# Products of constants in TensorE's known waits: a two-block kernel of hybrid attention, routed experts and a state-space branch

## The reference, cut to what matters

```python
def reference(...):
    x = first_block(...)     # (1, 512, 1024), context of 256 tokens
    return second_block(x, ...)

# first block
mod = silu(c) @ ada_w + ada_b
h = rmsnorm(x, g) * (1 + sc1) + sh1;  u = h @ w_in
a = diff_attention(u);  b = neighbourhood_attention(u);  p = pool_mix(u)
f = hyena_filters(S, w1, b1, w2, b2, w3, b3)
      # sin(z @ w1 + b1); sin(. @ w2 + b2); (. @ w3 + b3) * decay; normed
hy = hyena_mix(u, f)
x = x + g1 * (concat(a, b, p, hy) @ w_out)
h2 = rmsnorm(x, g2) * (1 + sc2) + sh2
x = x + g2 * moe(h2)         # 16 experts, the best 2 of the best group
x = rmsnorm(x, final_g)
# second block
h = rms_norm(x);  q, k, v, za, u, zs, g = split(h @ w_in_2)
attn = windowed_gqa(q, k, v) * silu(za)
ssm = s5_bidirectional(u) -> gelu -> glu -> * silu(zs)
merged = sigmoid(g_a) * (attn @ w_branch_attn) + sigmoid(g_s) * (ssm @ w_branch_ssm)
out = rms_norm(x + merged @ w_out)
```

## Time and profile before

| | us |
|---|---|
| median of 3 runs | 1337.29 |
| lowest and highest run | 1320.17, 1338.97 |
| the profiled execution | 1334.26 |
| its span, first to last instruction | 1332.2 |

### The profile page before, as it was taken

One profiled execution on the slowest core, in us unless ns is written; L12 is line 12 of the kernel. 1 busy time (PEld: TensorE's weight loads), 2 busy tenths in 40 slices (PEclk: granted clock), 3 DMA queues, 4 the chain that ended last, 5 costly groups with the idle time before them and its releaser, 6 DMA issues.

```text
span 1332.2 us, 16908 instructions
## 1 busy us (share of the span) xinstructions
PE 1220.0 (92%) x6412; PEld 899.1 (67%) x6412; DVE 862.2 (65%) x1282; ACT 588.6 (44%) x781; POOL 129.2 (10%) x126
## 2 busy tenths in 40 slices
PE   6999999968799995899999999889999898989996
PEld 1444474857688764788888888648877777765774
DVE  3479788768775447588898888664337555734543
ACT  1540010335555524487777787343333443334422
POOL 1101101000122000011221111300000000000000
PEclk9999999988799997899999999999999899899998
DMA  8735656770130053699999999652343445544301
GB/s 360 279 134 221 237 234 224 182 158 1 56 147 1 0 201 136 237 359 392 408 411 398 408 409 401 247 197 78 110 172 108 145 169 155 167 144 157 126 0 63
DMA packets 52822, 267.52 MB, mean 201 GB/s; under 512 B 15031, under 2 KB 22071, under 8 KB 38040
## 3 DMA queue, kind: packets, MB, share of 16 engines
q1 hardware_dynamic: 38264, 205.85, 42.1%
q0 software_dynamic: 9744, 47.19, 9.8%
q10 hardware_dynamic: 4752, 13.63, 2.7%
HBM read 226.80 MB, written 36.70 MB: 198 GB/s over the span
## 4 chain that ended last, share of the span: by engine, by line
PE 74%; DVE 13%; ACT 5%; DMA 3%; issue 3%; SPq 2%; POOL 1%; DVEq 0%; ACTq 0%; POOLq 0%
PE PS L2772 21%; PE PS L3196 7%; PE PS L3197 7%; PE PS L3198 7%; PE PS L3110 3%; PE PS L3422 3%; PE PS L3423 3%; PE PS L3424 3%; PE PS L3328 2%; PE PS L3327 2%; PE PS L3329 2%; PE PS L3064 2%; PE PS L3408 1%; SPq L804 1%; PE PS L2789 1%
## 5 line engine op out<-in xcount | busy, mean ns | idle before, releaser
L1394 ACT ACTIVATE arena_r<-ring 128x2048 fp32r<-128x2048 f32 x100 | 185.9, 1910 | 11.7 <-ACT arena L1431 7.4
L2772 PE MATMUL PS<-arena 128*128 128x64 f32 (+6 forms) x674 | 150.1, 390 | 30.0 <-DMA arena<-in_small_f_w 7.6
L2223 DVE TENSOR_TENSOR arena_r<-ring,arena_r 128x2048 fp32r<-128x2048 f32 x66 | 148.2, 2286 | 20.3 <-ACT arena_r L1394 19.7
L2772 PEld LDWEIGHTS PS<-arena 128*128 128x128 f32 (+2 forms) x674 | 100.2, 205 | 73.9 <-issue 40.5
L2772 PE MATMUL PS<-hT,ring 128*128 128x512 f32 (+1 forms) x304 | 118.9, 549 | 0.0
L3196 PE MATMUL PS<-arena_r,hT_r 128*128 128x512 f32 x272 | 112.4, 413 | 4.9 <-DVE hT_r L2405 4.9
L3422 PE MATMUL PS<-arena_r 128*128 128x512 f32 x256 | 104.7, 409 | 13.0 <-DVE ring_r L2631 8.5
L3197 PE MATMUL PS<-arena_r,hT_r 128*128 128x512 f32 x272 | 108.9, 400 | 0.0
L3424 PE MATMUL PS<-arena_r,ring_r 128*128 128x512 f32 x256 | 101.8, 398 | 0.0
L1203 ACT ACTIVATE arena<-PS 128x1024 f32<-128x1024 f32 (+2 forms) x31 | 28.5, 927 | 159.7 <-PE PS L2772 144.7
L2772 PEld LDWEIGHTS PS<-hT,ring 128*128 128x128 f32 x304 | 57.1, 190 | 59.0 <-issue 57.4
(11 more groups left out here) (481 smaller groups left out, 2416.0 us busy)
## 6 DMA issues: line engine op xcount, KB each, us to landing
ring<-in_moe SPq DMA_DIRECT2D x51, 2048.0 KB, 10.5
ring<-in_slabs SPq DMA_DIRECT2D x27, 2048.0 KB, 8.9
ring<-in_slabs SPq DMA_DIRECT2D x9, 1024.0 KB, 5.5
y_rows<-arena ACTq DMA_DIRECT2D x16, 512.0 KB, 10.0
ssm_scratch<-arena POOLq DMA_DIRECT2D x4, 1152.0 KB, 5.1
arena<-ssm_scratch POOLq DMA_DIRECT2D x4, 1152.0 KB, 8.3
ssm_scratch<-arena POOLq DMA_DIRECT2D x4, 1024.0 KB, 10.9
y_rows<-in_tab_no_token SPq DMA_DIRECT2D x1, 4096.0 KB, 25.1
```

The costliest lines, as they stand in the source:

```text
L1394: nc.scalar.activation(rounded(moe_w_hi[n][:, cols]), ring[:, n, cols], ACT.Copy).then_inc(s_moe_hi[n], 1)
L2223: nc.vector.tensor_tensor(rounded(moe_w_lo[n][:, cols]), ring[:, n, cols], as_float(moe_w_hi[n][:, cols]), ALU.subtract).then_inc(s_moe_lo ...
L2772: ins = nc.tensor.matmul(out, lhsT, rhs, start=(n == 0), stop=(n == len(pairs) - 1))
```

## The change

A helper issues `n` plain 32-bit products of `ones` by `vec` (256 columns) into a bank that is free at that point and is written anew by what follows. It is called ahead of waits of TensorE: before the second and the third filter layer (8, 4), before the list (7), before the first gathered rows and behind their transposes (11, 4), in the norms after the experts (2, 3), before the first of `ba`, `bs` and `o2` (2, 5, 4) and in the last norm (2, 2). At the very start 14 products of `ones` by `ones` (128 columns) come before the wait for the filter weights; TensorE now waits for `s_const` before them and for `s_small` behind them. The wait for the second sine moves behind `start_unit` of the first `f3` tile. Nothing else is changed on any engine.

```diff
+            def keep_clock(out, n):
+
+                for _ in range(n):
+                    nc.tensor.matmul(out[:, 0:NVEC], ones[:], vec[:], start=True, stop=True)
+
...
-            pe.wait_ge(s_filt_in, 64)
             key = ("f", 0)
             start_unit(key)
+            pe.wait_ge(s_const, 1)
+            for _ in range(14):
+                nc.tensor.matmul(bank(key, 0)[:, 0:P], ones[:], ones[:], start=True, stop=True)
+            pe.wait_ge(s_small, 64)
+            pe.wait_ge(s_filt_in, 64)
             products(bank(key, 0)[0:64, :], [(f_w[0:HY_EMB, 0:64], z_emb[0:HY_EMB])], last=True)
             key = ("f", 1)
             start_unit(key)
+            keep_clock(bank(key, 0), 8)
             pe.wait_ge(s_sin, 1)
             products(bank(key, 0)[0:64, :], [(f_w[:, 64:128], f_small[:, 1])], last=True)
             ada(0)
 
-            pe.wait_ge(s_sin, 2)
             for t in range(QT):
                 key = ("f3", t)
                 start_unit(key)
+                if t == 0:
+                    keep_clock(bank(key, 0), 4)
+                    pe.wait_ge(s_sin, 2)
...
             key = ("list",)
             start_unit(key)
+            keep_clock(bank(key, 1), 7)
             pe.wait_ge(s_hot, 1)
...
+            keep_clock(PS[:, 0, :], 11)
             pe.wait_ge(s_taken, 16)
             transpose_taken()
+            keep_clock(PS[:, 0, :], 4)
             moe_tile(0, 0)
...
             key = ("nt",)
             start_unit(key)
+            keep_clock(bank(key, 1), 2)
             read(pe, ("n3",))
...
             for n, key in enumerate((("n4",), ("nx",))):
                 start_unit(key)
+                if n == 0:
+                    keep_clock(bank(key, 1), 3)
                 pe.wait_ge(s_diag, n + 2)
...
                 key = (name, j)
                 start_unit(key)
+                if j == 0:
+                    keep_clock(bank(key, 0), {"ba": 2, "bs": 5, "o2": 4}[name])
...
             key = ("n5t",)
             start_unit(key)
+            keep_clock(bank(key, 1), 2)
             read(pe, ("n5",))
...
             key = ("n5d",)
             start_unit(key)
+            keep_clock(bank(key, 1), 2)
             pe.wait_ge(s_diag, 4)
```

## The result

The changed kernel takes 1323.13 us in the median of 20 runs (1319.67 to 1334.41), beside 1335.90 us for the kernel before on the same chip (20 runs, 1320.17 to 1342.91). The ratio is 0.9935, 95% interval [0.9913, 0.9956]: 8.7 us less, 5.9 to 11.6 by the interval. The ratio on record is not the quotient of the two medians, which lie 12.8 us apart; this text goes by the ratio. Ratios are formed without slow runs, which the measurement of experiments 1 and 3 has among its runs of before (four of 35). The profiled execution of the changed kernel takes 1320.51 us with a span of 1318.4, which is 13.8 us under the profiled execution of before.

A forecast was written before the change was run, and what follows sets the result against it. TensorE was taken as the bound, with 74% of the chain and 61 us lost to low clock. Terms -5.8 - 3.0 - 0.85 - 1.0 - 0 - 1.7 - 1.6 = -13.95 took 1334.26 to 1320.3 us; range 1306 to 1332.

The forecast's parts named there:

- Start: Filter layers to first spectra: faster layers 0, 1 and 3, GpSimd next to bind; -5.8 us, bounds -6.8 and -3.
- term of +1.0 for slow spectra: First spectra: may run partly at 1.2 GHz after TensorE's wait for VectorE; +1.0 us taken, bounds 0 and 2.5.
- Layer 3 does not hold the clock: Rival, third filter layer: clock falls after the first few products, layer takes 10 to 13 us; total -11, 1323; chance 0.20.
- List and experts: List and first expert: list -0.75 us, first expert's passes -2.2; together -3.0, bounds -4.5 and +1.5.
- L2405 is not delayed in either case: First gathered rows: 11 products, even started slow, take 7.2 us; transposes then take 1.03 instead of 1.97 us.
- Norms: Norms after the experts, -0.85 us, and last norm, -1.0: slow matmuls reach full clock; bounds 0 and -1.85 for both.
- Last branches: Ahead of ba, bs, o2: products fit waits and spare slow stretches; 0, -1.7 and -1.6 us, bounds 0 and -3.3.
- New dips: Rival: earlier phases bring new slow stretches, up to the 10 us of attention; -4 in all, 1330 us; chance 0.15.
- more dips gone: Rival, the opposite across the kernel: some 12 us more than the sum by the runs' spread, 1308 us; chance 0.11.
- The range: Whole kernel: 1306 to 1332 us, from bounds plus the runs' spread of some 9 us to either side.
- sum of bounds: Whole kernel, good direction: -6.8 - 4.5 - 1.85 - 3.3 = -16.5 us, giving 1318.
- rule of the Trainium skill: Whole kernel: ramp penalty under 1% of span, so slow stretches worth under 13.3 us and an estimate above 1321.

The follow-up runs named there:

- experiments 1 and 3: Changed kernel with only, or without, the start's products (ratios 0.9984, 0.9997); changed kernel with none or ten products ahead of bs (0.9946, 0.9961).
- after: The changed kernel itself in its first profile, against the kernel before: median 1323.13 us, ratio 0.9935, profiled span 1318.4 us.
- before_a: The kernel before, unchanged, profiled a second time: 1329.17 us in one run.
- no_start_b: Second profile of the changed kernel without the start's three groups of products: 1324.78 us in one run.
- best: Changed kernel with seven edits, mainly moving products into waits, none ahead of bs, slab 3 loaded earlier: 1317.07 us, ratio 0.9857 to the kernel before.
- best_two: best with 8 products added in ada_tr(2) and 8 for 6 ahead of ba: 1328.81 us, ratio 0.9955 to the kernel before.
- start_only: Changed kernel with every kept product dropped but the start's 14, 8 and 4: 1325.86 us, ratio 0.9984 to the kernel before.
- after_b: The changed kernel, unchanged, profiled and timed again on another chip: 1321.43 us, ratio 0.9897 to the kernel before.
- no_start: Changed kernel without the start's 14, 8 and 4 products, later ones kept: 1329.76 us, ratio 0.9997 to the kernel before.

## Why the prediction came out as it did

The time was forecast as 1320.3 us and is 1323.13; the profiled pair differs by 13.8 us for 13.95 forecast. That nearness is partly luck. The direction and most mechanisms were right; one place had the wrong sign, and the start was priced from one draw. Point by point, with the interval means in place of a single pair:

- **Start, forecast -5.8.** Right for layers 0 and 1 (-1.7 together for -1.9), for layer 3 (7.13 us, ending at 25.7), for GpSimd as next, and nearly for `ada_tr(2)`: VectorE freed its bank by 37.0 as computed, but `ada(3)`, behind a slab whose landing I had not looked up, held it to 37.87. Up to there the forecast was -6.8; the pair has -6.0, the means -4.6. What was mis-sized is layer 3: its price at the low level was read from an execution in which it was largest. The term of +1.0 for slow spectra measured 0: they ran partly at the low level in seven of the 14 profiles (7.96 to 8.34 us for 7.03), as feared, and the interval from the third L1740 to the next L1783 is 13.09 to 13.11 us in all 14: the chain runs through ScalarE's squares there, which hide them. The rest of the pair's -9.2 is a dip of before at 62 us that after did not have: from that L1783 to the first of the next pass it is 20.7 us in before and 17.4 in after, 17.4 to 20.7 in the others, with products in the start or without.
- **Layer 3 does not hold the clock (1323).** Falls with the products: nine of nine profiles at 7.13 us. Without them it is what happened in `before_a` and `no_start_b`. The measured median is this rival's 1323, but not for its reason.
- **List and experts, forecast -3.0.** List 1.06 us long, -0.6 for -0.75. First tile: D goes from 27.3 to 25.0, -2.3 for -2.2. The step that failed is "L2405 is not delayed in either case": the 11 products end at 520.9, not at the 7.2 us after the start that I gave them but at 7.6, L2405 then waits 0.66 us for ScalarE's copy of the late transposes, and C grows from 4.8 to 5.5 in the mean of the seven profiles with 11 products (4.82 to 5.73), +0.7. Sum -2.2. With seven products, C is 4.77 again.
- **Norms, forecast -0.85 and -1.0.** From L2453 to the first L2483 the mean of before is 16.2 us (15.79 to 16.53), after and six others with the products have 15.50: -0.7. The products are not the whole of it: `best` and `best_two` have them too and 16.01. H: -1.07.
- **Last branches, forecast 0, -1.7, -1.6.** `bs` is the plain miss: +2.17. I read the 2.81 us wait of the earlier trace rows as the one ahead of `bs`'s first product because it was a row of the right line and near the right time. Counting matmuls would have shown it: it is ahead of the 85th of `ba`'s 96. `o2` is right in size (G: 30.9 to 29.4, -1.5) for a partly wrong reason: its products run before the unit and not in the long wait, and G in `start_only` is as short without them.
- **New dips, more dips gone.** Both exist in single executions: I spans 198.2 to 207.5 us over 14 profiles with no tie to the edits that these few profiles show.
- **The range.** The sum of bounds gives 1318, and 9 us below it is 1309; the low end of 1306 doesn't follow from it. Nothing measured hangs on this.

The sum of means is -5.2 - 2.2 - 0.7 + 2.2 - 1.5 - 1.1 = -8.5 us. The first measured ratio says -8.7 (5.9 to 11.6 us less), the second, of `after_b` on another chip, -13.8 (9.1 to 18.4 less). The two intervals share 9.1 to 11.6. So the nearness of 8.5 and 8.7 proves little, and by the second measurement the forecast of -13.95 would be right and the sum short; E, where both profiles of the changed kernel have 3.84 us for 5.4, is not in it, being held for a draw. The forecast was 5.4 us better than the sum of means, of which 3.9 are the sign of `bs`, 0.6 the start and 0.8 the overrun. Of the rule of the Trainium skill that the prediction set against the trace (TensorE: Matmul & The Clock Gate, "The HAM clock gate", under 1% of the span): its sentence is on the ramp, and the prediction stretched it to all slow stretches. The profiles here have mean clocks of 0.950 to 0.969, 3 to 5% lost by the clock row. That is a share of the clock, waits of TensorE included, and not time on the path. What the section says of a count that varies from run to run, the five values of layer 3 bear out.

What stays open: what sets where the clock falls inside I; why the two measurements of the changed kernel differ by 5 us; the 4.5 us of `best_two`; and how much of each of `ba`'s and the second block's products helps, since the profiles without them are sometimes as fast.

## What to carry to other kernels

Products that keep the clock belong inside the wait that cools the engine: find it by counting instructions from the start of the unit, look up which call holds it (the bank's or the data's), and put them ahead of that call. Behind it each costs 0.43 us on the path. Take their number from the low level's price (0.44 a matmul here) if they start cold, and price such a change from several profiles of the kernel before, by intervals between the same two instructions: one pair gave 9.2 us for a place that is worth about 5.

## What the runs showed that was not expected

- The same instructions get another clock in another execution: layer 3 at 7.13, 11.88, 12.57 and 14.02 us.
- VectorE's sums of 128x512 took 2.53 and 2.83 us while GpSimd multiplied, 0.67 after it. By these rows that is 4.0 us of VectorE's time in the start. It isn't so for every instruction: its biases (L1758, read from PSUM) took 1.23 us beside a multiply in the changed kernel and 1.22 with GpSimd idle in before. No run tried to part the two engines.
- 14 us of back-to-back 64-row products did not raise the clock in two executions of before, and in `before_a` and `no_start_b` it fell among them. In nine profiles with products ahead, and in `no_start` without, it held for all 7 us.
- Slow matmuls off the path are free: the spectra's extra 0.9 to 1.3 us left no trace in the interval that follows them.
